# Second attentions two heads at a time, by feature, and the two norms behind the output projection

## What is computed

```python
h = _modulate(_rmsnorm(x, g_mix), shift_mix, scale_mix)
q_d, k_d, v_d, q_s, k_s, v_s = split(h @ w_in)
o_dil = _dilated_mixture(q_d, k_d, v_d)          # softmax attention with a bias per head and distance
o_sb  = _stick_breaking_attention(q_s, k_s, v_s)
mixed = concatenate([_rmsnorm(o_dil, g_dil_out), _rmsnorm(o_sb, g_sb_out)])
x = x + gate_mix * (mixed @ w_out)
...
# stick breaking, for each head, z = q k^T / 8, keys s before query t:
log_keep = where(causal, log_sigmoid(-z), 0)
between  = cumsum(log_keep, reverse=True) - log_keep
weights  = where(causal, exp(log_sigmoid(z) + between), 0)
out      = weights @ v
```

## Time and profile before

| | us |
|---|---|
| median of 3 runs | 3680.25 (3675.88 to 3687.18) |
| profiled execution | 3682.91, its span 3681.7 |
| attention stage of the second block | 2171.4 to 2747.0 of the span |
| mix | 2747.0 to 2780.5 |
| output projection | 2780.5 to 2893.2 |
| TensorE busy over the span | 3103.3 (84%) |
| VectorE, ScalarE, GpSimd busy | 1179.4 (32%), 680.4 (18%), 291.2 (8%) |
| mean granted TensorE clock | 0.902 of full |

### The profile page before, as it was taken

The page is one execution under the profiler, slowest core; times in us unless marked ns, Lnnn a source line. Parts: engine busy times, 40 slices in busy tenths (PEclk is TensorE's granted clock), DMA queues, the critical chain, the costliest instruction groups (busy, mean ns, idle before and its releaser), DMA issues.

```text
span 3681.7 us, 32460 instructions
## 1 busy us (share of the span) xinstructions
PE 3103.3 (84%) x12500; PEld 1568.5 (43%) x12500; DVE 1179.4 (32%) x2845; ACT 680.4 (18%) x1549; POOL 291.2 (8%) x311
## 2 busy tenths in 40 slices
PE   4987999997859999996199998888888769999971
PEld 3536844443533333332144455665654433333320
DVE  4008944345431111111600025555542431111105
ACT  2113610000201111110400013333331211111112
POOL 0000000000011010100400001111100010111004
PEclk9997999998969999998599989989888879999985
DMA  6203023325159779884601000000011169899984
GB/s 238 92 0 109 2 69 115 114 91 197 57 204 378 309 306 399 354 352 182 223 26 46 23 0 1 1 0 1 1 54 40 46 256 388 349 402 356 382 320 145
DMA packets 177789, 609.81 MB, mean 166 GB/s; under 512 B 59490, under 2 KB 101986, under 8 KB 152932
## 3 DMA queue, kind: packets, MB, share of 16 engines
q1 hardware_dynamic: 112692, 531.35, 36.7%
q0 software_dynamic: 64944, 76.38, 6.3%
HBM read 556.75 MB, written 50.60 MB: 165 GB/s over the span
## 4 chain that ended last, share of the span: by engine, by line
PE 75%; DMA 11%; DVE 9%; ACT 2%; issue 2%; POOL 1%; SPq 1%; POOLq 0%; DVEq 0%; ACTq 0%
PE ps L1575 15%; DMA R<-in_w_up 8%; PE ps L1553 7%; PE ps L1024 6%; PE ps L918 6%; PE ps L1928 6%; PE ps L436 3%; PE ps L1925 3%; PE ps L922 3%; PE ps L2108 2%; PE ps L2123 2%; PE ps L733 2%; PE ps L2115 2%; PE ps L2139 2%; PE ps L2130 2%
## 5 line engine op out<-in xcount | busy, mean ns | idle before, releaser
L1575 PE MATMUL ps<-R 128*64 128x512 f32 x1520 | 729.6, 625 | 82.1 <-DMA R<-in_w_up 78.7
L1576 PE MATMUL ps<-R 128*64 128x512 f32 x1520 | 729.9, 626 | 0.0
L1575 PEld LDWEIGHTS ps<-R 128*64 128x64 f32 x1520 | 208.0, 143 | 502.1 <-issue 493.4
L1553 PE MATMUL ps<-R 128*64 128x512 f32 x1520 | 342.4, 592 | 1.0 <-DVE R L1448 1.0
L1448 DVE COPY R<-ps 128x256 f32<-128x256 f32 x95 | 40.3, 424 | 686.7 <-PE ps L1537 686.7
L1024 PE MATMUL ps<-R 128*128 128x512 f32 x512 | 231.6, 616 | 20.9 <-DMA R<-in_w_o 19.6
L918 PE MATMUL ps<-R 128*128 128x512 f32 x512 | 229.3, 607 | 0.5 <-ACT R L712 0.5
L1928 PE MATMUL ps<-R 128*128 128x512 f32 x512 | 222.8, 598 | 3.2 <-issue 3.2
L1576 PEld LDWEIGHTS ps<-R 128*64 128x64 f32 x1520 | 207.9, 143 | 0.0
L1553 PEld LDWEIGHTS ps<-R 128*64 128x64 f32 x1520 | 108.8, 137 | 217.4 <-issue 216.1
L1461 DVE TENSOR_TENSOR R<-ps,R 64x512 f32<-64x512 f32 x95 | 64.9, 683 | 343.7 <-ACT R L1499 188.2
(11 more groups left out here) (291 smaller groups left out, 4030.0 us busy)
## 6 DMA issues: line engine op xcount, KB each, us to landing
R<-in_w_gate SPq DMA_DIRECT2D x64, 2048.0 KB, 13.2
R<-in_w_up SPq DMA_DIRECT2D x64, 2048.0 KB, 13.9
R<-in_w_down SPq DMA_DIRECT2D x64, 2048.0 KB, 19.6
R<-in_w_ada SPq DMA_DIRECT2D x40, 1024.0 KB, 5.4
R<-in_w_in SPq DMA_DIRECT2D x13, 2048.0 KB, 8.4
YE<-R POOLq DMA_DIRECT2D x64, 256.0 KB, 22.9
YE<-acc POOLq DMA_DIRECT2D x33, 256.0 KB, 22.5
R<-in_w_ada SPq DMA_DIRECT2D x4, 2048.0 KB, 16.0
```

Source lines behind the costliest of these rows:

```text
L1553: i_ = T.matmul(k.ps[64 * hf:64 * hf + 64, 5 + b % 2, :], v.hT[b % 2][:, kk, :], v.down[n % RING][:, kk, 512 * hf:512 * hf + 512], start=k ...
L1575: T.matmul(k.ps[64:128, b % 2, :], x_, wg[:, kk, :], start=kk == 0, stop=kk == 7)
L1576: i_ = T.matmul(k.ps[0:64, b % 2, :], x_, wu[:, kk, :], start=kk == 0, stop=kk == 7)
```

## The change

Steps are replaced by 48 units and 32 tasks, both for two heads 2c and 2c + 1 at once. A unit is a stick-breaking key block kb against the half Q of the queries (at most 512 columns). A task is a dilated query block. Task m is scored in the iteration that `SCORED_AT` names and turned and multiplied by v in that of `VALUED_AT`, so two tasks run in three iterations, and every third iteration has none. The two heads' scores use the two row halves of the array, each with a PSUM bank of its own; the products with v take v as stationary operand (64 columns) and write the two heads to partitions 0 to 63 and 64 to 127, up to 512 columns (units) or 128 (tasks), so results `oT` lie by feature. |z| is one bitwise VectorE instruction; max(z, 0) and the sum are one. 1/sum is applied to the probabilities by a new GpSimd instruction ahead of the transposes. One PSUM bank (`T_BANK`) holds a task's transposes, first head 0's, copied out by VectorE, then head 1's, copied by ScalarE, and then its product.

The transposes and scalings of the mix are gone. The gains are multiplied into w_out by GpSimd in iterations 40 to 47; w_out and x are loaded in pieces during the attention. The projection runs on the unnormalised `oT`, dilated and stick-breaking sums in two PSUM banks, and both are scaled by their 1/root behind it: one ScalarE and three VectorE instructions for each of 16 groups. The squares are taken by feature (ScalarE and VectorE, four instructions each), and their sums over the features by 64 matmuls of one column, put behind the second group. The router's weights are loaded to `acc`. In the expert loop seven semaphores become three, with the same waits.

```diff
+def units():
+    rows = []
+    for c in range(4):
+        for Q in range(2):
+            for kb in range(4 * Q + 3, -1, -1):
+                a = max(128 * kb, 512 * Q)
+                rows.append((c, Q, kb, a, 512 * Q + 512 - a, kb >= 4 * Q, kb == 4 * Q + 3, kb == 0))
+    return rows
+TASKS = [(c, qd) for c in range(4) for qd in (0, 7, 1, 6, 2, 5, 3, 4)]
+PARTS = [1 if qd < 4 else 2 for _, qd in TASKS]
+SCORED_AT = {3 * m // 2: m for m in range(ND)}
+VALUED_AT = {(3 * (m + 1)) // 2: m for m in range(ND)}
 def tensor_pairs(k):
...
+        m, w = SCORED_AT.get(n), VALUED_AT.get(n)
+        if m is not None:
+            score_part(m, 0)
+        if 1 <= n <= NU:
...
+            T.wait_ge(s["a_w"].sem, 2 * n)
...
+            for x in range(2):
+                h = 2 * c + x
+                i_ = T.matmul(k.ps[64 * x:64 * x + 64, O_BANK, a - 512 * Q:512], v.v2[1][:, kb, 64 * h:64 * h + 64],
+                              v.EA[(n - 1) % 3][x][:, 0:N], start=first, stop=last, skip_group_check=True)
...
+            for x in range(2):
+                P0 = 64 * x
+                i_ = T.matmul(z_row(k, n + 1, x), v.kT[1][P0:P0 + 64, c, 128 * kb:128 * kb + 128],
+                              v.qT[1][P0:P0 + 64, c, a:a + N], start=True, stop=True)
...
+        if m is not None and PARTS[m] == 2:
+            score_part(m, 1)
+        for x in range(2):
+            if w is not None:
+                turn(w, 0, x)
+            if 0 <= n < NU:
+                sums(n, x)
...
+                for x in range(2):
+                    turn(w, 1, x)
+            c, qd = TASKS[w]
+            T.wait_ge(s["v_pa"].sem, PARTS_BY[w + 1])
+            T.wait_ge(s["a_pa"].sem, PARTS_BY[w + 1])
             for j in range(qd + 1):
...
+                    i_ = T.matmul(k.ps[64 * x:64 * x + 64, T_BANK, 0:128], v.v2[0][:, j, 64 * h:64 * h + 64],
+                                  v.PA[x][:, 128 * j:128 * j + 128], start=j == 0, stop=j == qd)
 def vector_pairs(k):
...
+                V.tensor_scalar(v.EA[(n + 1) % 3][x][:, 0:UNITS[n + 1][4]].bitcast(I32), z.bitcast(I32), 0x7FFFFFFF,
+                                None, ALU.bitwise_and).then_inc(*s["v_abs"].up())
...
+                i_ = V.scalar_tensor_tensor(lp[:, 0:N], z_row(k, n + 1, x), 0.0, v.EA[(n + 1) % 3][x][:, 0:N],
+                                            ALU.max, ALU.add)
 def gpsimd_pairs(k):
...
+                G.tensor_scalar(sa, sa, k.dsm[m0 % 2][x][:, 4:5], None, ALU.mult).then_inc(*s["g_p"].up())
 def scalar_mix(k):
...
+    for c in range(4):
+        S.activation(squares_of(k, 0)[c], v.oT[0][:, c, :], ACT.Square).then_inc(*s["a_mix"].up())
...
+    for n in range(16):
...
+        S.mul(k.R0[:, 512 * (n % 2):512 * (n % 2) + 512], k.ps[:, 2 * (n % 3), :], k.rs16[:, n // 2:n // 2 + 1]
+              ).then_inc(*s["a_mix"].up())
 def vector_mix(k):
...
+        V.scalar_tensor_tensor(t, k.ps[:, 2 * (n % 3) + 1, :], k.rs16[:, 8 + i:9 + i], t, ALU.mult, ALU.add
+                               ).then_inc(*s["v_mix"].up())
...
+        V.tensor_tensor(t, t, k.g1b[:, 512 * h2:512 * h2 + 512], ALU.mult).then_inc(*vo.up())
...
+        V.tensor_tensor(x_, x_, t, ALU.add).then_inc(*vo.up())
 def tensor_mix(k):
...
+        if n == 2:
...
+            for a in range(2):
+                for j in range(8):
+                    for c in range(4):
+                        i_ = T.matmul(k.ps[:, T_BANK, 8 * a + j:8 * a + j + 1],
+                                      squares_of(k, a)[c][:, 128 * j:128 * j + 128], k.ones[:, 0:1], start=c == 0,
+                                      stop=c == 3)
```

More of the change, by code:

```diff
@@ L154, in setup @@
     k.wts = [(small(8), small(8)) for _ in range(2)]
-    k.dsm = [small(3) for _ in range(3)]
+    k.dsm = [[small(5) for _ in range(2)] for _ in range(2)]
+    k.ss16, k.rs16 = small(16), small(16)
     k.gdc, k.gsc = small(4), small(4)
@@ new lines, in score_part, with turn @@
+    def score_part(m, j):
+        c, qd = TASKS[m]
+        n = min(128 * (qd + 1) - 512 * j, 512)
+        T.wait_ge(s["v_s"].sem, 2 * (PARTS_BY[m] + j))
+        for x in range(2):
+            P0 = 64 * x
+            i_ = T.matmul(k.ps[:, S_BANK + x, 0:n], v.qT[0][P0:P0 + 64, c, 128 * qd:128 * qd + 128],
+                          v.kT[0][P0:P0 + 64, c, 512 * j:512 * j + n], start=True, stop=True)
+        i_.then_inc(*s["p_s"].up())
+    def turn(m, g, x):
+        _, qd = TASKS[m]
+        if g == 0:
+            T.wait_ge(s["g_p"].sem, 2 * m + x + 1)
+        if x == 0 and g == 0 and m:
+            T.wait_ge(s["v_do"].sem, m)
+        if x == 0 and g:
+            T.wait_ge(s["a_pa"].sem, PARTS_BY[m] + g)
+        if x:
+            T.wait_ge(s["v_pa"].sem, PARTS_BY[m] + g + 1)
+        for j in range(4 * g, min(qd + 1, 4 * g + 4)):
+            i_ = T.transpose(k.ps[:, T_BANK, 128 * (j - 4 * g):128 * (j - 4 * g) + 128],
+                             v.SA[m % 2][x][:, 128 * j:128 * j + 128], k.ident)
+        i_.then_inc(*s["p_tp"].up())
@@ new lines, in sums @@
+    def sums(n, x):
+        c, Q, kb, a, N, diag, first, last = UNITS[n]
+        z, lp = z_row(k, n, x), v.LP[n % 2][x]
+        T.wait_ge(s["v_lp"].sem, LP_BY[n] + (x + 1) * (2 if diag else 1))
+        i_ = T.matmul(z, k.C("nge"), lp[:, 0:N], start=False, stop=first and not diag, skip_group_check=True)
+        if not first:
+            o = 128 if diag else 0
+            T.wait_ge(s["g_ls"].sem, SUMS_BY[n - 1] - 1 + x)
+            i_ = T.matmul(z[:, o:N], k.C("neg"), v.LS[x][:, a - 512 * Q + o:512], start=False, stop=not diag,
+                          skip_group_check=True)
+        if diag:
+            i_ = T.matmul(z[:, 0:128], k.ident, k.C("ngm"), start=False, stop=True, skip_group_check=True)
+        i_.then_inc(*s["p_cum"].up())
@@ L2217, in scalar_mix @@
[L2217 to L2235 removed]
+    V.wait_ge(s["v_so"].sem, 8)
@@ new lines, in vector_mix @@
+    V.wait_ge(s["p_pv"].sem, NU)
+    V.wait_ge(s["p_do"].sem, ND)
+    for c in range(4):
+        V.tensor_tensor(squares_of(k, 1)[c], v.oT[1][:, c, :], v.oT[1][:, c, :], ALU.mult).then_inc(*s["v_mix"].up())
+    V.wait_ge(s["p_ss"].sem, 1)
+    V.tensor_scalar(k.ss16, k.ps[:, T_BANK, 0:16], 1.0 / 512, EPS, ALU.mult, ALU.add).then_inc(*s["v_mix"].up())
+    V.wait_ge(s["a_mix"].sem, 5)
+    V.reciprocal(k.rs16, k.ss16).then_inc(*s["v_mix"].up())
+    V.wait_ge(s["v_mix"].sem, 6)
+    V.wait_ge(s["v_row"].sem, 2)
```

530 lines of the change are left out of this document (257 added, 273 removed).

## The result

The changed kernel takes 3523.51 us (median of 4 runs, 3521.0 to 3533.36), the kernel before on the same chip 3678.07 us (median of 4): the ratio is 0.958, interval 0.956 to 0.961. The profiled execution took 3521.0 us, its span 3519.8.

The account below looks back on a forecast made before the run. TensorE was taken to bound the attention stage, with hand-offs of about a sixth. Profiled 3682.9 us, less 136 for that stage (575.6 to 440), plus 0 for mix and projection, gave 3547 us; range 3480 to 3615.

Parts of the forecast that it names:

- What bounds the stage: Attention stage, 575.6 us: TensorE bounds it, with 408 us of work at full clock and hand-offs of about a sixth.
- idle ahead of z: Attention stage before the change: TensorE idle 131 us ahead of z, for ScalarE's last exp and VectorE's copy.
- Work taken off TensorE: Attention stage: head pairs on array halves cost one; z and scores 123 to 61 us, products 131 to 62.
- Rival (a): Attention stage: row halves or short column pairs don't overlap; stage 475 to 501 us, time 3582 to 3608, chance 0.12.
- the doubt whether products on the same rows hide their loads: Products with v: by a skill rule, column halves sharing rows hide no weight loads; short pairs would give 35 us more.
- The changes of form: Attention stage: some 170 switches between column halves, row halves and whole array at 0.10 us each, 17 us in all.
- The walk: Attention stage, one period of three iterations timed: 24.3 us, 17.3 of it work; 112 us idle over the stage.
- The clock: Attention stage: TensorE's granted clock stays at 0.88 or a little below, taking 406 us at full clock to 440.
- Rival (d): Attention stage: half-array pairs with idle between keep the clock at the low level; 613 us, time 3720, chance 0.04.
- VectorE, ScalarE, GpSimd: Attention stage loads: VectorE 243 us, ScalarE 225, GpSimd below 170; none bounds by its sum, their order matters.
- Rival (b): Attention stage: hand-offs or clock worse than walked, engines chained through one transpose bank; 488 us, time 3595, chance 0.15.
- Mix and projection: Behind attention: the mix's 33.5 us are handed back in full, 154 against 153.8 us; nil, from -15 to +5.

Follow-up runs that it names:

- e1: Changed kernel with TensorE's order product of head 0, z of head 0, then both of head 1, so pairs never stand together: 3622.67 us, stage 102 us longer.
- e2: Changed kernel with each pair of z matmuls issued twice in a row: 3572.59 us, stage 458.6 us.
- e10: Changed kernel with a task's product of head 0 over all key blocks, then head 1, so short pairs are split: 3537.52 us, stage 439.8 us.
- e7: Changed kernel with GpSimd's multiplication by 1/sum done on one column of each row only: 3526.36 us, stage 420.5 us.
- e4: Changed kernel with ScalarE's exps of a large task moved behind the last unit's weights, VectorE's 1/sum behind its |z|: 3515.11 us, stage 410.2 us.
- e5: Changed kernel with both the early VectorE copy of head 0's transposes (e3) and the late ScalarE exps (e4): 3508.98 us, stage 402.2 us.
- e8: e5 with VectorE's copy of a finished task product also put ahead of its |z|: 3487.09 us, stage 388.1 us.
- e3: Changed kernel with VectorE's copy of head 0's transposes ahead of the row maxima of a large task's second part: 3529.65 us, stage 430.7 us.
- e9: e8 plus sums over 16 one-column matmuls and ScalarE's squares of x between its projection scalings: 3473.24 us, 0.943 of the kernel before.

## Why the prediction held, point by point

*What bounds the stage.* Right. e1, e2 and e10 add work to TensorE and get it back as time, 102, 38 and 19 us; e7 takes 91 us from GpSimd and gets nothing. No run takes work from VectorE or ScalarE; that neither sets the pace by its sum rests on TensorE's added work being paid in full, while e4, e5 and e8 show that the order of theirs does matter. One figure of the reading was wrong: the 131 us "idle ahead of z" adds the waits of matmuls and of weight loads, which overlap, and so came out larger than the 86 us that the same paragraph leaves for all idle time; by the rows TensorE ran no matmul for 70.5 us.

*Work taken off TensorE.* Right in each pair: rows (e2), long columns (e1) and short columns (e10) cost one. Rival (a) is out, and so is the doubt whether products on the same rows hide their loads: pairs of 128 columns stand 0.109 us apart. The changes of form cost 0.15 to 0.20 us each where I read them, not 0.10, and so some 170 of them, as an estimate, about 27 us, not 17.

*The walk.* It gave 277 + 17 + 112 = 406 us at full clock. Measured: 420.8 us at a mean clock of 0.95 is 400 at full clock if all of the loss is on the path. The total was right to 2%, in part by luck: the changes of form were 10 us dearer, and what is left for idle, some 96 us, is 16 less than walked. The waits that it named are those of the trace (VectorE's copy, ScalarE's weights), and it missed one, TensorE's wait for the copy of the last product, 16.8 us.

*The clock.* This is the term that was mis-sized. I let it stay at 0.88 since the share of work was the same, and added 34 us for it; it was 0.95 and the loss at most 0.05 x 420.8 = 21. That is 13 of the 19 us by which the stage was shorter than 440. The runs show that it moves by a few hundredths with the order alone, 0.93 in e3, 0.97 in e4, 0.98 in e9, and that this is worth as much as the waits themselves. Rival (d), the low level throughout, did not come.

*VectorE, ScalarE, GpSimd.* 243, 225 and 106 to 163 us were worked out; 230, 205 and 206 measured. Of the 206 the multiplications by 1/sum are 110, where 34 to 91 stood, and w_out's gains 23, where I had 8 to 20 beside the sum. (Rival (b) speaks of five engines at 225 to 277 us; by its own sums there are three, TensorE, VectorE and ScalarE.) GpSimd's scaling is the one price that lay outside its bounds: 2.84 us for 1024 columns, where the adds' 2.52 was my upper end and the memset's 0.95 the one I leaned to. The step that failed is the choice of the nearest row: one tensor input doesn't make it like a memset. It cost nothing in the changed kernel, as e7 shows.

*Mix and projection.* I had 154 us to the route stage's work against 153.8. Measured by the first normalised row 147.2 against 152.9. The one-column matmuls took 23.3 us where 30 stood. Nearly a third of them ran before the clock fell, at 0.11 us a record, and the others took 0.21; the first block's 0.233 had another source, and why it was dearer stays open. Behind them the clock was low up to 2630, some 2 us lost, 3 predicted. The tail grew by 3.5 us, 3.1 predicted. That the mix's 33.5 us would be all but handed back held, with 6 us left over.

*What e1 and the others price.* Of the 155 us saved in the stage, 131 at most are work, as worked out: z and scores 62 and the products 69. The rest, 24 us, is the better clock (69 us lost before, 21 now, if all of it was on the path) less the idle time and the changes of form, 99 us before and some 123 now. What the work is worth was tested from the changed kernel by e1, e2 and e10; the difference of idle and clock was only read from the two traces.

## What to carry to other kernels

Where heads have 64 features, put two on the two halves of the array, next to each other in TensorE's list and, as here, in separate banks or partitions: scores by row halves, products with the values stationary and the weights streamed by column halves. A pair costs one at 512 columns and at 128, and a change of form between pairs cost 0.15 to 0.20 us here. Before moving one instruction for a wait, look at what waits behind it on its engine, and try the mends together as well as singly: here the same move cost 10 us alone and gave 8 in company. And look at the granted clock of the stage that follows: in two profiled runs here, time gained ahead of a stretch of short matmuls was lost in it.

## What was not expected of the hardware

- The clock fell during the one-column matmuls although TensorE was busy all the time: 1.00 for 3.9 us, then 0.56, then 0.50 for the other 18.7 us, and 0.21 us a record in place of 0.11.
- Through transposes and 36-column matmuls it can stay down: after the 0.93 of the 5.2 us gap in e9 the router ran 41 us at 0.50, busy throughout; in the changed kernel, which waited 10.2 us at a mean of 0.75, it rose to 1.00 within 6 us. The traces of two kernels show the one and those of eleven the other; what decides stays open.
- GpSimd's multiplication of a row by a scalar of its partition took 2.84 us for 1024 fp32 columns, more than its addition of two tensors (2.52).
